# Gated delta net prologue: gate rows loaded first, squares split over two engines, activations grouped by function, no barriers between the parts

## What is computed

```python
def l2norm(t):
    return t * lax.rsqrt(jnp.sum(t * t, axis=-1, keepdims=True) + EPS)
...
    qh, kh, vh = l2norm(heads(qc)), l2norm(heads(kc)), heads(vc)
    beta = jax.nn.sigmoid(beta_pre...)
    g = -jnp.exp(a_log) * jax.nn.softplus(alpha_pre + dt_bias)
...
    gc = jnp.cumsum(g.reshape(b, h, nc, L), axis=-1)
    q_dec = q * jnp.exp(gc)[..., None]
    k_state = k * jnp.exp(g_last[..., None] - gc)[..., None]
```

## Time and profile before

| | us |
|---|---|
| median of three runs | 4466.06 |
| profiled execution | 4472.06 |
| its span | 4470.7 |
| TensorE busy in the span | 3989.1 (89%) |
| VectorE | 2031.7 (45%) |
| ScalarE | 1269.1 (28%) |
| GpSimd | 447.0 (10%) |

### The profile page before, as it was taken

One profiled execution on the slowest core, in us unless ns is written; L12 is line 12 of the kernel. 1 busy time (PEld: TensorE's weight loads), 2 busy tenths in 40 slices (PEclk: granted clock), 3 DMA queues, 4 the chain that ended last, 5 costly groups with the idle time before them and its releaser, 6 DMA issues. The chain is left out here.

```text
span 4470.7 us, 75771 instructions
## 1 busy us (share of the span) xinstructions
PE 3989.1 (89%) x33550; PEld 3231.1 (72%) x33550; DVE 2031.7 (45%) x3326; ACT 1269.1 (28%) x1819; POOL 447.0 (10%) x442
## 2 busy tenths in 40 slices
PE   6999938986898899999899999778888899999979
PEld 5788827774676688888678677556666678888857
DVE  4633325554333444444522322455544365665662
ACT  4222244432222321212311233242323232222231
POOL 0001102231201000000100000231311200000010
PEclk8999868997899899999999999888778999999989
DMA  5211110113112111111132322211004211111101
GB/s 183 83 47 60 52 66 16 31 31 140 43 38 94 38 47 47 48 57 48 42 112 85 125 86 81 76 39 50 22 9 162 84 39 47 57 46 40 57 31 64
DMA packets 213691, 282.00 MB, mean 63 GB/s; under 512 B 15580, under 2 KB 170972, under 8 KB 213236
## 3 DMA queue, kind: packets, MB, share of 16 engines
q1 hardware_dynamic: 176048, 185.58, 13.2%
q10 hardware_dynamic: 37316, 91.56, 5.4%
HBM read 217.11 MB, written 60.00 MB: 62 GB/s over the span
## 5 line engine op out<-in xcount | busy, mean ns | idle before, releaser
L429 PE MATMUL ps<-sb_a_h,sb_whi 128*128 128x512 f32 (+1 forms) x3008 | 1215.6, 404 | 132.9 <-DVE sb_a_h L523 66.3
L430 PE MATMUL ps<-sb_a_h,sb_wlo 128*128 128x512 f32 (+1 forms) x3008 | 1193.4, 397 | 0.0
L431 PE MATMUL ps<-sb_a_h,sb_whi 128*128 128x512 f32 (+1 forms) x3008 | 1193.3, 397 | 0.0
L429 PEld LDWEIGHTS ps<-sb_a_h,sb_whi 128*128 128x128 f32 (+1 forms) x3008 | 575.9, 191 | 304.8 <-issue 107.2
L431 PEld LDWEIGHTS ps<-sb_a_h,sb_whi 128*128 128x128 f32 (+1 forms) x3008 | 577.2, 192 | 124.9
L430 PEld LDWEIGHTS ps<-sb_a_h,sb_wlo 128*128 128x128 f32 (+1 forms) x3008 | 578.3, 192 | 118.8 <-issue 2.9
L390 DVE TENSOR_TENSOR sb_wlo<-sb_wraw,sb_whi 128x2048 fp32r<-128x2048 f32 (+3 forms) x146 | 314.9, 2157 | 330.0 <-ACT sb_whi L382 304.6
L1900 DVE TENSOR_TENSOR sb_x<-sb_x,ps 128x512 f32<-128x512 f32 x480 | 314.4, 684 | 298.0 <-PE ps L431 297.8
L382 ACT ACTIVATE sb_whi<-sb_wraw 128x2048 fp32r<-128x2048 f32 (+3 forms) x146 | 260.4, 1783 | 659.8 <-PE ps L431 490.8
L429 PE MATMUL ps<-sb_a_g,sb_whi 128*128 128x512 f32 x896 | 349.7, 390 | 9.5 <-DVE sb_x L1900 9.5
L431 PE MATMUL ps<-sb_a_g,sb_whi 128*128 128x512 f32 x896 | 348.7, 389 | 0.0
(11 more groups left out here) (486 smaller groups left out, 5425.3 us busy)
## 6 DMA issues: line engine op xcount, KB each, us to landing
sb_wraw<-w_in SPq DMA_DIRECT2D x33, 1024.0 KB, 5.3
sb_wraw<-w_ff SPq DMA_DIRECT2D x32, 1024.0 KB, 5.3
sb_wraw<-w_up SPq DMA_DIRECT2D x22, 1024.0 KB, 5.1
sb_wraw<-w_down SPq DMA_DIRECT2D x11, 1024.0 KB, 4.9
sb_wraw<-w_xkv SPq DMA_DIRECT2D x8, 1024.0 KB, 5.5
sb_wraw<-w_out SPq DMA_DIRECT2D x8, 1024.0 KB, 5.5
sb_a_f<-y ACTq DMA_DIRECT2D x16, 512.0 KB, 4.9
gates<-sb_a_f ACTq DMA_DIRECT2D x32, 256.0 KB, 2.0
```

What stands on the lines that cost most here:

```text
L429: e.matmul(o, wh[:, k, c], xh[:, sl], start=(k == 0), stop=False)
L430: e.matmul(o, wl[:, k, c], xh[:, sl], start=False, stop=False)
L431: m = e.matmul(o, wh[:, k, c], xl[:, sl], start=False, stop=(k == t.nk - 1))
```

## The change

Five things, all in `gdn`:

1. ScalarE issues only the gate rows' DMA. SyncE issues `gd_qkv` in three DMAs of three tiles each (q, k, v), each with a semaphore of its own.
2. Squares have six buffers, roots six. ScalarE squares tiles 0, 2, 4 after the softplus `Ln`; VectorE squares tiles 1, 3, 5 after the decay. The summing matmuls use all eight banks (`ALL`).
3. ScalarE does the twelve `Ln` of the unit rows one after another, then the six `Exp`, then the three small `Exp` of the gates. For the last, VectorE first copies two of the chunk sums out of PSUM (L1443).
4. VectorE's 16 small copies stand behind its six multiplications.
5. The barrier between unit rows and turning is gone. All v groups are turned first, then all k groups; the k groups wait for the last multiplication (`un_done.at(5)`), the v groups for the third DMA.

```diff
             def ac_in(e):
-                e.dma_start(R(QKV, 9 * T).rearrange("p (k t) -> p k t", k=9),
-                            S["gd_qkv"].rearrange("(k p) t -> p k t", p=128)).then_inc(*gd_in.up())
-                e.dma_start(R(X0, T, 0, 24), S["gd_g"]).then_inc(*gd_in.up())
+                e.dma_start(R(X0, T, 0, 24), S["gd_g"]).then_inc(*gd_gin.up())
+
+            def sp_in(e):
+                for j in range(3):
+                    e.dma_start(R(QKV + 3 * j * T, 3 * T).rearrange("p (k t) -> p k t", k=3),
+                                S["gd_qkv"][384 * j:384 * (j + 1), :].rearrange("(k p) t -> p k t", p=128)).then_inc(*gd_in[j].up())
+
+            def pe_unit_row(e, f):
+                for hf in range(2):
+                    ps = bk.take(("gd_un", f, hf), ALL)
+                    e.wait_ge(*un_squared[f % 2].at(f // 2))
+                    e.wait_ge(*bk.room(("gd_un", f, hf)))
+                    e.matmul(ps, C("blk"), un_sq[f][:, hf * 512:(hf + 1) * 512], start=True,
+                             stop=True).then_inc(*bk.fill(("gd_un", f, hf)))
...
                 m.then_inc(*bk.fill("gd_sums"))
+                for f in range(6):
+                    pe_unit_row(e, f)
...
                                        ALU.mult, ALU.mult).then_inc(*gd_decay.up())
+                for f in (1, 3, 5):
+                    q = R(QKV + f * T, T)
+                    e.wait_ge(*gd_in[f // 3].at(0))
+                    e.tensor_tensor(un_sq[f], q, q, ALU.mult).then_inc(*un_squared[1].up())
...
-                e.tensor_tensor(g96[KSF], bk["gd_sums"][:, 192:288], g96[GC], ALU.subtract).then_inc(*gd_diff.up())
+                e.tensor_tensor(g96[KSF], bk["gd_sums"][:, 192:288], g96[GC], ALU.subtract).then_inc(*vo.up())
+                e.tensor_copy(R(G0 + 96 * EGL, 192), bk["gd_sums"][:, 0:192]).then_inc(*bk.empty("gd_sums"))
+                for f in range(6):
+                    src = R(QKV + f * T, T)
+                    e.wait_ge(*un_root.at(f))
+                    e.tensor_tensor(src, src, un_rt[f], ALU.mult).then_inc(*un_done.up())
...
-                e.wait_ge(*gd_diff.at(0))
+                for f in (0, 2, 4):
+                    e.wait_ge(*gd_in[f // 3].at(0))
+                    e.activation(un_sq[f], R(QKV + f * T, T), ACT.Square).then_inc(*un_squared[0].up())
+                for f in range(6):
+                    for hf in range(2):
+                        e.wait_ge(*bk.filled(("gd_un", f, hf)))
+                        e.activation(un_rt[f][:, hf * 512:(hf + 1) * 512], bk["gd_un", f, hf], ACT.Ln, bias=EPS,
+                                     scale=1.0).then_inc(*bk.empty(("gd_un", f, hf)))
+                for f in range(6):
+                    for hf in range(2):
+                        e.wait_ge(*bk.emptied(("gd_un", f, hf)))
+                    e.activation(un_rt[f], un_rt[f], ACT.Exp, scale=-0.5, bias=LN8 if f < 3 else 0.0).then_inc(*un_root.up())
...
-            pe_unit_rows(pe), ac_unit_rows(ac), ve_unit_rows(ve)
-            next_phase()
-
-            turns = [(i, dst, f0) for i in range(8) for dst, f0 in ((kTM, 3), (vTM, 6))]
+            turns = [(i, dst, f0) for dst, f0 in ((vTM, 6), (kTM, 3)) for i in range(8)]
 
             def pe_turn(e):
                 for n, (i, dst, f0) in enumerate(turns):
                     ps = bk.take(("gd_turn", n), RING)
+                    e.wait_ge(*(un_done.at(5) if f0 == 3 else gd_in[2].at(0)))
                     e.wait_ge(*bk.room(("gd_turn", n)))
```

More of the change, by code:

```diff
@@ L1374, in gdn @@
             ESJ = g96[10].rearrange("p (k d q) -> p k d q", k=16, d=2)
+            un_sq = [R(X0 + (1 + f) * T, T) for f in range(6)]
+            un_rt = [R(H0 + f * T, T) for f in range(6)]
+            ALL = tuple(range(8))
             def ac_in(e):
-                e.dma_start(R(QKV, 9 * T).rearrange("p (k t) -> p k t", k=9),
-                            S["gd_qkv"].rearrange("(k p) t -> p k t", p=128)).then_inc(*gd_in.up())
-                e.dma_start(R(X0, T, 0, 24), S["gd_g"]).then_inc(*gd_in.up())
+                e.dma_start(R(X0, T, 0, 24), S["gd_g"]).then_inc(*gd_gin.up())
[10 more added lines that the diff above has]
+                             stop=True).then_inc(*bk.fill(("gd_un", f, hf)))
             def pe_gates(e):
                 ps = bk.take("gd_gates", RING)
-                e.wait_ge(*gd_in.at(1))
+                e.wait_ge(*gd_gin.at(0))
                 e.wait_ge(*bk.room("gd_gates"))
@@ L1419, in ve_gates @@
                 e.wait_ge(*bk.filled("gd_sums"))
-                e.tensor_tensor(g96[KSF], bk["gd_sums"][:, 192:288], g96[GC], ALU.subtract).then_inc(*gd_diff.up())
+                e.tensor_tensor(g96[KSF], bk["gd_sums"][:, 192:288], g96[GC], ALU.subtract).then_inc(*vo.up())
[4 more added lines that the diff above has]
+                    e.tensor_tensor(src, src, un_rt[f], ALU.mult).then_inc(*un_done.up())
                 e.wait_ge(*gd_exps.at(1))
                 e.tensor_tensor(g96[BG], g96[BE], g96[EGC], ALU.mult).then_inc(*vo.up())
-                e.wait_ge(*bk.emptied("gd_sums"))
+                e.wait_ge(*gd_exps.at(2))
                 for b in range(2):
@@ L1448, in ac_gates @@
+                for f in range(6):
+                    for hf in range(2):
+                        e.wait_ge(*bk.emptied(("gd_un", f, hf)))
+                    e.activation(un_rt[f], un_rt[f], ACT.Exp, scale=-0.5, bias=LN8 if f < 3 else 0.0).then_inc(*un_root.up())
+                e.wait_ge(*bk.emptied("gd_sums"))
                 e.activation(g96[KSF], g96[KSF], ACT.Exp).then_inc(*gd_exps.up())
                 e.activation(g96[EGC], g96[GC], ACT.Exp).then_inc(*gd_exps.up())
-                e.activation(R(G0 + 96 * EGL, 192), bk["gd_sums"][:, 0:192], ACT.Exp).then_inc(*bk.empty("gd_sums"))
@@ L1452, in gdn @@
[L1452 to L1487, removed]
-            pe_unit_rows(pe), ac_unit_rows(ac), ve_unit_rows(ve)
-            next_phase()
-            turns = [(i, dst, f0) for i in range(8) for dst, f0 in ((kTM, 3), (vTM, 6))]
+                e.activation(R(G0 + 96 * EGL, 192), R(G0 + 96 * EGL, 192), ACT.Exp).then_inc(*gd_exps.up())
@@ L1494, in pe_turn @@
+            sp_in(sp), ac_in(ac), pe_gates(pe), ve_gates(ve), ac_gates(ac)
+            turns = [(i, dst, f0) for dst, f0 in ((vTM, 6), (kTM, 3)) for i in range(8)]
             def pe_turn(e):
@@ L1884, in program @@
         na_av, na_exp, na_rec, na_prob = (sig(f"na_{n}") for n in ("av", "exp", "recip", "prob"))
-        gd_in, gd_pre, gd_log, gd_decay, gd_diff, gd_exps = dma_sig("gd_in"), sig("gd_pre"), sig("gd_log"), sig("gd_decay"), sig("gd_diff"), sig("gd_exps")
-        un_squared, un_root, un_done = sig("unit_squared"), sig("unit_root"), sig("unit_done")
+        gd_gin, gd_in, gd_pre, gd_log, gd_decay, gd_exps = dma_sig("gd_gates_in"), [dma_sig(f"gd_in{j}") for j in range(3)], sig("gd_pre"), sig("gd_log"), sig("gd_decay"), sig("gd_exps")
+        un_squared, un_root, un_done = [sig(f"unit_squared{j}") for j in range(2)], sig("unit_root"), sig("unit_done")
         gd_x0, gd_xa0, gd_mask, gd_dec = ([sig(f"gd_{n}{d}") for d in range(2)] for n in ("x0_", "xa0_", "mask", "decay"))
```

2 lines of the change are left out of this document (1 added, 1 removed).

## The result

The changed kernel took 4440.85 us, the median of seven runs (4421.96 to 4447.41), against 4467.07 us (4464.67 to 4471.19) for the kernel before. The ratio is 0.9929, 95% interval 0.9915 to 0.9944: by the interval 25 to 38 us faster, while the two medians lie 26.2 apart. In a second set of runs the same two kernels gave 4425.41 and 4466.82 us, a ratio of 0.9904 (0.9886 to 0.9922). The forecast was 4429.6 us, with a range of 4421 to 4443: the measured median lies inside it, 11.3 us above the forecast.

A forecast was written before the change was run, and what follows sets the result against it. TensorE bounds the kernel, but this stage between barriers adds its length one for one. Gains of 10.9 us (earlier start), 25.6 (unit rows) and nothing (turning) make 36.5, taking the median 4466.06 to 4429.6 us; range 4421 to 4443.

The forecast's parts named there:

- the early gates: Loading: gate rows on their own queue land at 583.7 instead of releasing TensorE at 594.91; softplus logarithm ends at 589.1.
- the wait on bank 0: Start of unit sums: VectorE empties bank 0 only behind its three squares, so TensorE starts at 594.3, 3 us of gain lost.
- the one table load: Unit rows: one load of 1.28 us between the last logarithm and the first exponential, where twelve loads stood before.
- the late small copies: End of prologue: 2.0 us of gate product and copies now lie behind the multiplications, until 619.3, ahead of VectorE's turning copies.
- The clock of the sums: Twelve unit sums: 5 us at 1.2 GHz, then 2.4 GHz, 12.8 us in all; ends 11.7 and 20.5 us.
- Rival A: Unit sums: clock stays at 1.2 GHz, costing 7.7 us there and 0.5 in turning, total 4437.8 us; chance 0.10.
- Rival B: Loading: gate rows land with the rest at 594.9, unit sums start 11.0 us later, total 4440.6 us; chance 0.07.
- up to 2.6 us more: Loading: estimated delay of the gate rows if DMA engines drain a packet of the other queue before changing over.
- 10.9 us to the earlier start: Loading and gates: unit sums start at 594.3 instead of 605.2, a gain of 10.9 us.
- 25.6 to the unit rows: Unit rows, sums through multiplications: 25.6 us of the 36.5 us gain.
- Rival C: Loop: TensorE's clock stays at 0.50 and pays the gain back; 80 us of it gives 4493 us; chance 0.05.
- a median may be off by about 3: Range: three runs of before spread over 6.5 us, so a median was allowed an error of about 3 us.

The follow-up runs named there:

- v1: Changed kernel with the unit sums' eight banks taken from bank 1 on, bank 0 last: prologue 41.8 us, total 4421.17 us (0.9908 to before).
- u3: Changed kernel with all six squares on ScalarE, VectorE's three deleted: prologue 43.8 us, total 4422.44 us (0.9895 to before).
- v2: v1 plus k before q, k groups turned from the third multiplication, eight turning banks, other copy shares: 4421.36 us (0.9915), again 4420.82 us (0.9895).
- v3: v2 with small exponentials ahead of the large ones, gate product and 16 small copies on GpSimd: prologue 38.5 us, total 4415.61 us (0.9896 to before).

## Why the prediction was right

By its own steps, in microseconds from the first DMA issue:

| step | predicted | measured |
|---|---|---|
| gate rows release TensorE | 3.6 | 2.35 |
| softplus logarithm ends | 9.0 | 7.7 |
| k tiles landed | 11.0 | 10.4 |
| unit sums start | 14.2 | 13.6 |
| unit sums take | 12.8 | 13.45 |
| first large exponential starts | 29.1 | 29.1 |
| last multiplication ends | 37.2 | 37.2 |
| TensorE starts the last ten groups | 39.8 | 39.8 |
| ten groups take | 5.9 | 5.2 |
| the loop starts | 46.8 | 46.0 |

The mechanism is the one forecast: the early gates, the wait on bank 0, the one table load and the late small copies stand in the timeline where the prediction put them. That some lines agree to a tenth is in part luck: the unit sums began 0.6 us early and took 0.65 us longer, and so ended at 27.0 us, as forecast.

**The bank.** The hidden wait on bank 0 was in the sum, and v1 and u3 show that it was real: changing nothing but the order of eight banks took it away. The list of instructions of the changed kernel shows it ahead of any run.

**The clock of the sums.** I took 5 us at 1.2 GHz; it was 6, for the sums had begun at 590.07:

```profile
594.00:596.00 2.00, 2.00 (x3) 0.67 (x2) 0.00 (x0) 0.98 (x2) 0.00 (x0) 0.51 0.00 0
596.00:598.00 2.00, 2.00 (x6) 0.95 (x5) 0.00 (x0) 1.39 (x3) 0.00 (x0) 1.00 0.00 0
```

Rival A, no rise at all, fell in every trace: the sums never took more than 13.5 us.

**The gate rows.** They landed apart from the large load. They were issued on another queue, and also 0.01 us ahead of it; which of the two did it, no run separates, for the loading undone changed both. Rival B fell: 2.35 us is even shorter than the 3.0 us of the 96 KB row. By the Trainium skill ("DMA: Bandwidth & Descriptors", Queues, rings and completion order) a packet of the other queue could have gone first. The prediction's estimate of that was up to 2.6 us more; no trace here shows such a delay. Of the 1.3 us by which the step came earlier than in my sum, half was left at the start of the unit sums (13.6 for 14.2), since VectorE's second square waited for the k tiles (0.91 us idle).

**The table loads.** The traces have no case of one load serving both functions: the changed kernel has a load between its last `Ln` and its first `Exp`, and with the grouping undone there were two a tile again. In the tile shown with the grouping undone, the second logarithm ends at 604.48, the load runs from 604.55 to 605.83, and the exponential starts at 605.85: a change of function cost 1.28 us and 0.09 us around it.

**By place.** The prediction gave 10.9 us to the earlier start, 25.6 to the unit rows and nothing to turning. Measured between the same points, the start of the unit sums came 11.5 us earlier (25.1 us after the first issue before, 13.6 now), from there to the last multiplication it is 25.2 us shorter (48.8, now 23.6), and turning is 0.6 shorter (9.4, now 8.8). Undone one at a time, by the length of the prologue, the loading is worth 11.0 us, the grouping 11.2, the removed barrier 0.6 and the split of the squares -2.2. That leaves some 17 us of 37.3 for the opened chain (six buffers, squares ahead, the sums in one row), which no experiment took away by itself; parts undone from a whole need not add up, so this is a remainder and not a measurement. It fits the traces, though: a tile took 8.0 us before and 5.1 with the chain open and the grouping undone, which is 17.4 us on six tiles.

**The total.** Rival C didn't happen as told: the loop took 379.0 us in the one trace of before and 369.8 to 382.3 in the twelve others. What it names, a loop whose length goes with TensorE's clock, is there in a smaller size and in both directions. The step of the prediction that was too narrow is "a median may be off by about 3": I took it from three runs of before that lay within 6.5 us. Between the two traces of the changed kernel, with the same prologue, the span moved by 20.6 us, and 18.4 of these lie in the loop and in the second block's mixers, where the granted clock differed. The kernel before, in the later sets, spread as well (4457 to 4474, 4454 to 4471, 4462 to 4479). The medians lie 26.2 us apart in one set and 41.4 in the other, on the two sides of the 37.3 that the prologue shows; its ratio, 0.9917, is inside both intervals.

Each version's median less its own prologue says where the miss lies. It is 4377 to 4388 us in fifteen of the sixteen sets of runs, those of before and of the changed versions alike, and 4395 in the first set of the changed kernel. So the 11.3 us by which the forecast was missed are of that set and lie behind the prologue; the 36.5 us of the sum were 37.3. That the median still fell inside the range is in part luck: the upper end of 4443 was set by rivals A and B, and neither came.

**What is left.** Two versions stand out by their traces: the bank order alone (41.8 us of prologue, one tuple) and v2 (37.7 and 37.9). Against before, v2 measured 0.9895 and 0.9915. Against the changed kernel the 8 us can't be told in the totals: on the same chip and in the same set they were 4420.82 and 4425.41 us.

## What to carry to other kernels

When an instruction list is split over two engines, look at what stands behind the new work in the second engine's list: here three squares on an idle VectorE sat ahead of the copy that frees a bank, and TensorE paid for it. In a chain of small steps, first let each engine run ahead over all tiles (buffers and banks for it), and only then ask which function changes remain; undone alone, the grouping was worth 10 to 11 us of 37. And where single executions differ by more than the gain, judge a local change by the length of its own stage in the trace, and use totals only for the sign.

## What the runs showed of the hardware

Executions of one and the same kernel differ, and with them the granted clock of TensorE, in stages of many small matmuls: 369.8 us at 0.94 and 381.3 us at 0.91 for the same loop. What sets the one or the other was not found.

GpSimd's small copies took five times as long while VectorE multiplied. In v3, the timeline of both engines:

```profile
605.42 0.20 POOL L1463 COPY sb_b<-sb_b 64x24 f32<-64x24 f32 x1
605.68 0.21 POOL L1461 COPY sb_b<-sb_b 64x24 f32<-64x24 f32 x1
605.78 6.98 DVE L1449 TENSOR_TENSOR sb_b<-sb_b 128x1024 f32<-128x1024 f32 x6 [13.35 <-ACT sb_b L1497]
605.96 1.12 POOL L1463 COPY sb_b<-sb_b 64x24 f32<-64x24 f32 x1
607.14 1.08 POOL L1468 COPY sb_b<-sb_b 64x24 f32<-64x24 f32 x1
...
612.89 0.21 POOL L1463 COPY sb_b<-sb_b 64x24 f32<-64x24 f32 x1
```

While the six multiplications ran (605.78 to 612.76) each copy took 1.1 us, about the length of one of them, and before and after it 0.2. VectorE hardly noticed (6.98 us for 6.90). The Trainium skill ("SBUF — State Buffer", Who interferes with whom) says that a VectorE instruction with two inputs in SBUF contends with a GpSimd instruction that reads SBUF, and that the ports they share are an exclusive lock. This trace agrees, with 1.1 us for 0.2.
